# Four of the twelve output groups of the adaLN modulation computed on VectorE instead of TensorE

## The chip, the cores and the metric

One Trainium2 chip, one of its cores. The time is that of one execution on the device in microseconds (us), the median of the runs of a kernel. All data are float32, and the whole reference runs in one launch.

## The reference, cut to what matters

The program is a hybrid mixer block (gated linear attention, mLSTM, S5, SwiGLU) followed by two more layers (latent attention, LRU). The change touches the first step only: the modulation vector from the condition `c`, and beside it the first RMS norm.

```python
# c: (1, 1024), ada_w: (1024, 6144), ada_b: (6144,)
mod = silu(c) @ ada_w + ada_b            # six vectors of 1024: shift1, scale1, gate1, shift2, scale2, gate2
h = rms_norm(x, pre1_w) * (1 + scale1) + shift1       # x: (1024 tokens, 1024 features)
```

The product is a vector times a matrix of 25 MB. Only the first two of the six vectors (mod 0 to 15 below) are needed by the first norm; the others are used much later. Independent of both, keys and values of a memory of 256 tokens are computed from the input `mem_2`.

## The kernel before, in words

**Layout.** Features lie on the 128 partitions. `mod` is a tile of 128 x 48: column m holds outputs 128m to 128m+127. `ada_w` arrives in 48 slots of 512 KB. Slot n holds 256 rows of the matrix (k = 0, 1: two times 128 rows) for 512 columns; four slots make a group g = n // 4 of 512 outputs, which is four columns of `mod`. A ring `ada_w` holds eight slots.

**The product before.** DVE spreads silu(c) to `act0_wide` (L948), 128 equal columns for each block of 128 rows. TensorE multiplies (L932) each half slot by it, 128 x 128 stationary and 128 x 512 moving, and adds eight such products up in a PSUM bank (0 and 1 by turns). All 128 rows of the bank then hold the same 512 outputs. DVE multiplies them by the identity repeated four times (`pick`, L958) and sums along the free axis (L962) into four columns of `mod`. TensorE may enter the bank of group g only when the pick of group g - 2 is done. A float32 matmul stands in the trace as two MATMUL and two LDWEIGHTS rows, so that a slot is four rows of L932.

**What runs beside it.** `side_by_side` (L499) merges the programs of several parts into one instruction order for each engine: each `yield` names a due time, and instructions are issued in the order of due times; afterwards each engine follows that fixed order and waits on semaphores. S(n) = 8 + 1.9n is the due time of slot n and X(i) = S(2 + 5i) that of quarter i of x. The parts are these.

- `modulation()`: the above. SyncE issues the transfer of slot n when slot n - 8 has been used (`pe_done`).
- `first_slots()`: six slots of the ordinary weight ring `w`; ACT rounds four of them (L268), and GpSimd subtracts to get the rest (L277).
- `squares()`: four transfers of 1 MB of x (L1002), ACT squares (L1014), DVE adds up over the features (L1024), in two halves of 512 tokens.
- `statistic()` for each half: TensorE sums over the partitions with narrow products (L784: four products of 128 x 128 by 128 x 1), DVE and ACT make the root, and TensorE spreads it over a bank with two rows of L791.
- `normed()` for each half: DVE scales x (L1039), ACT adds the shift and rounds (L1051), DVE makes the rest (L1043), eight tiles each. It needs `fold`, which needs mod 0 to 15, groups 0 to 3.
- `memory_keys()`: when the last L1043 is done, since it lies over x, SyncE loads `mem` (L1073); ACT rounds (L1125), DVE makes the rest (L1151). TensorE's work on it (L285 with `mem_parts`) stands behind all 48 slots in TensorE's order.

The next stage begins when this block has ended on every engine.

**Lines that matter in the order of DVE.** Before the change, DVE's order from the pick of group 3 on is: that pick, mod and fold (L965, L953, L967), the last seven adds of L1024 among the sixteen pairs of L1039 and L1043, and a pick for each further group wherever its due time falls.

Of the kernel before, what the change touches and what calls it, by code (L numbers as in the profile page):

```python
# [24 lines left out]
ALU = mybir.AluOpType  # L25
AX = mybir.AxisListType

P = 128
# [3 lines left out]
HALF = 512  # L32
# [3 lines left out]
ADA_RING = 8  # L36
ADA_SLOTS = 48
# [94 lines left out]
def ordered(*programs):  # L132

    waiting = [[next(p, None), n, p] for n, p in enumerate(programs)]
    waiting = [w for w in waiting if w[0] is not None]
    while waiting:
        first = min(waiting, key=lambda w: w[:2])
        yield first[0]
        at = next(first[2], None)
        if at is None:  # L140
            waiting.remove(first)
        else:
            assert at >= first[0] - 1e-6, (at, first[0])
            first[0] = at
# [10 lines left out]
def build(nc, a):  # L155
    ctx = ExitStack()
    with ctx:
# [3 lines left out]
        def sb_in(scope, name, shape, dt=F32, high=False):  # L161

            names[name] = names.get(name, 0) + 1
            name = f"{name}_sb{names[name]}"
            size = -(-int(np.prod(shape[1:])) * 4 // 32) * 32
            edges = sorted(spans)
            holes = list(zip([SBUF_LO] + [e for _, e in edges], [b for b, _ in edges] + [SBUF_HI]))
            fits = [(lo, hi) for lo, hi in holes if hi - lo >= size]
            assert fits, (name, size, holes)
            at = (fits[-1][1] - size) // 32 * 32 if high else fits[0][0]  # L170
            span = (at, at + size)
            spans.append(span)
            scope.callback(spans.remove, span)
            return nc.alloc_sbuf_tensor_at(name, shape, dt, offset=at)
# [20 lines left out]
        def sem(name):  # L195
            return Count(ctx.enter_context(nc.semaphore(name)))
# [5 lines left out]
        def over(counts):  # L202

            for count, times in counts:
                spare.append(Count(count.sem, count.n + times))

        ps = ctx.enter_context(nc.psum_tensor("ps", [P, 8, HALF], F32))
# [7 lines left out]
        mod = sb("mod", [P, 48])  # L215
        fold = sb("fold", [P, 32])
        act0 = sb("act0", [P, 8])
# [9 lines left out]
        ident, ones = C("ident"), C("ones")  # L227
# [4 lines left out]
        pe_done = sem("pe_done")  # L232
        act_free = sem("act_free")
        dve_free = sem("dve_free")
        ada_full = [sem(f"ada_full{s}") for s in range(ADA_RING)]
# [658 lines left out]
        with ExitStack() as scope:  # L894
            ada_w = sb_in(scope, "ada_w", [P, ADA_RING, 2, HALF])
            pick = sb_in(scope, "ada_pick", [P, 4, P])
            act0_wide = sb_in(scope, "ada_silu", [P, DT, P])
# [4 lines left out]
            silu_s, wide_s, picked, fold_s = sem("ada_silu"), sem("ada_wide"), sem("ada_picked"), sem("ada_folded")  # L902
            x_s = [sem(f"x0_loaded{i}") for i in range(4)]
            sq_s, acc_s, scaled_s, hi_s, lo_s = (sem("norm1_squares"), sem("norm1_sums"), sem("norm1_scaled"),
                                                 sem("norm1_hi"), sem("norm1_lo"))
            base = pe_done.n

            S = lambda n: 8.0 + 1.9 * n
            X = lambda i: S(2 + 5 * i)

            def modulation():
                def on_sp(sp):
                    yield -10.0
                    sp.dma_start(vec[:], a["vec"]).then_inc(loaded.sem, 16)
                    sp.dma_start(cst[:], a["cst"]).then_inc(loaded.sem, 16)
                    for n in range(ADA_SLOTS):
                        yield S(n - ADA_RING) + 2.1
                        if n >= ADA_RING:
                            sp.wait_ge(pe_done.sem, base + n - ADA_RING + 1)
                        sp.dma_start(ada_w[:, n % ADA_RING].rearrange("p k m -> p (k m)"), a["ada"][n]  # L920
                                     ).then_inc(ada_full[n % ADA_RING].sem, 16)

                def on_pe(pe):
                    for n in range(ADA_SLOTS):
                        yield S(n)
                        if n == 0:
                            pe.wait_ge(wide_s.sem, 1)
                        if n % 4 == 0 and n >= 8:
                            pe.wait_ge(picked.sem, n // 4 - 1)
                        pe.wait_ge(ada_full[n % ADA_RING].sem, 16 * (n // ADA_RING + 1))  # L930
                        for k in range(2):
                            mm = nc.tensor.matmul(ps[:, n // 4 % 2], act0_wide[:, 2 * (n % 4) + k],  # L932
                                                  ada_w[:, n % ADA_RING, k], start=(n % 4 == 0 and k == 0),
                                                  stop=(n % 4 == 3 and k == 1))
                        mm.then_inc(pe_done.sem, 1)

                def on_act(act, link):
                    yield 0.0
                    act.wait_ge(loaded.sem, 32)
                    nc.scalar.activation(act0[:], V("c", 0, 8), ACT.Silu).then_inc(silu_s.sem, 1)  # L940
                    yield S(ADA_SLOTS)
                    act.wait_ge(pe_done.sem, base + ADA_SLOTS)
                    nc.scalar.activation(act0[:, 1:2], act0[:, 1:2], ACT.Copy).then_inc(act_free.sem, 8)

                def on_dve(dve, link):
                    yield 0.2
                    dve.wait_ge(silu_s.sem, 1)
                    nc.vector.tensor_copy(act0_wide[:], act0[:].unsqueeze(2).broadcast_to([P, DT, P])  # L948
                                          ).then_inc(wide_s.sem, 1)

                    def folded(weights):
                        for j, (w, m) in weights:
                            link(nc.vector.scalar_tensor_tensor(fold[:, 8 * j:8 * j + 8], mod[:, m:m + 8], 1.0, V(w, 0, 8),  # L953
                                                                ALU.add, ALU.mult))
                    for g in range(ADA_SLOTS // 4):
                        yield S(4 * g + 4) + 0.6
                        dve.wait_ge(pe_done.sem, base + 4 * g + 4)
                        nc.vector.tensor_tensor(pick[:], ps[:, g % 2].rearrange("p (j m) -> p j m", m=P),  # L958
                                                ident.unsqueeze(1).broadcast_to([P, 4, P]), ALU.mult
                                                ).then_inc(picked.sem, 1)  # L960
                        dve.wait_ge(picked.sem, g + 1)
                        link(nc.vector.tensor_reduce(mod[:, 4 * g:4 * g + 4], pick[:], AX.X, ALU.add))  # L962
                        if g == 3:

                            link(nc.vector.tensor_tensor(mod[:, 0:16], mod[:, 0:16], V("ada_b", 0, 16), ALU.add))  # L965
                            folded([(0, ("pre1_w", 8))])
                            nc.vector.tensor_copy(act0[:, 2:3], act0[:, 2:3]).then_inc(fold_s.sem, 1)  # L967
                    link(nc.vector.tensor_tensor(mod[:, 16:48], mod[:, 16:48], V("ada_b", 16, 32), ALU.add))
                    folded(enumerate([("post1_w", 16), ("pre2_w", 32), ("post2_w", 40)], 1))
                    nc.vector.memset(act0[:, 0:1], 0.0).then_inc(dve_free.sem, 8)  # L970
                return Part(on_sp, on_pe, on_act, on_dve)

            def first_slots():
                at = lambda n: S(8 + 4 * (n - RAW)) if n >= RAW else -1.0 + n
# [194 lines left out]
            for h in range(2):  # L1169
# [1 line left out]
                root = statistic(at, total[:, tokens(h)], [(acc_s.sem, 7 * h + 7)], (2 + h,), D, dg[:, h], st[:, h])  # L1171
                parts += [root, normed(h, max(at + 8.0, S(16) + 5.0), root.done, 2 + h)]
            side_by_side(modulation(), first_slots(), squares(), *parts)
            pe_done.n += ADA_SLOTS
            act_free.n += 8
            dve_free.n += 8
            loaded.n += 32
            stream["slot"] += 8
            kv_written.n += 64
            over([(mem_s, 16), (mem_hi, 8), (mem_lo, 8), (one_s, 2), (kv_t, 8), (slot_t, 0), (k_taken, 4), (v_taken, 4)])  # L1180
            over([(silu_s, 1), (wide_s, 1), (picked, ADA_SLOTS // 4), (fold_s, 1), (sq_s, 16), (acc_s, 14), (scaled_s, 16),
                  (hi_s, 16), (lo_s, 16), *((x, 16) for x in x_s)])
        x0_scope.close()
        kv_scope = ctx.enter_context(ExitStack())
# [1370 lines left out]
        with ExitStack() as scope:  # L2555
# [19 lines left out]
            def sums(dve, link):  # L2575
                for n, (m, hs) in enumerate(LATE_HALVES[1:], 1):
                    yield mixed.job_end[(m, hs)] + 0.8
                    cols = slice(hs[0] * HALF, (hs[-1] + 1) * HALF)
                    dve.wait_ge(*sq_s.at(n + 1))
                    if n > 1:  # L2580
                        dve.wait_ge(*acc_s.at(n - 1))
                    nc.vector.tensor_tensor(total[:, cols], total[:, cols], sq[:, n % 2, cols], ALU.add
                                            ).then_inc(acc_s.sem, 1)
# [1561 lines left out]
```

## Time and profile before

| | |
|---|---|
| median of three runs | 3388.56 us (3388.53 to 3395.3) |
| the profiled execution | 3396.56 us, of which the span from first to last instruction is 3394.4 us |
| granted TensorE clock, mean over the span | 0.940 |
| PE / DVE / ACT / POOL busy over the span | 91% / 39% / 29% / 24% |
| transfer of `ada_w` | 48 x 512 KB, median 6.6 us from issue to landing |

TensorE is busy nearly everywhere. The part of the program that is changed takes about the first 106 us of the span. PE, DVE, ACT, POOL and SP are TensorE, VectorE, ScalarE, GpSimd and SyncE; times in the rows are us from the span's start, mean durations of one instruction ns.

### The profile page before, as it was taken

The page shows a single profiled execution, that of the slowest core. Times are in us where ns is not written, and L with a number is a line of the kernel's source. Part 1 is how long each engine was busy: PE and PEld are TensorE (multiplying, and loading weights), DVE is VectorE, ACT ScalarE, POOL GpSimd, SP SyncE. Part 2 cuts the span into 40 slices and gives each one's busy share as a digit, 9 for nine tenths or more (in the row PEclk, how much of TensorE's full clock was granted, in tenths as well). Part 3 has the DMA queues.
Part 4 walks back from the last instruction along what each step waited for, and adds up shares of the span by engine and source line. Part 5 has one row for each costly group of instructions (what it writes and reads, how often), then busy time and mean ns, then how long its engine had stood idle before and what let it go on. Part 6 is the DMA issues. An engine that isn't in the chain of part 4 may idle for free. (4 is left out here: it accounts for less than half of the span.)

```text
span 3394.4 us, 33644 instructions
## 1 busy us (share of the span) xinstructions
PE 3078.6 (91%) x14024; PEld 2303.9 (68%) x14024; DVE 1318.3 (39%) x1342; ACT 975.2 (29%) x1262; POOL 813.6 (24%) x380
## 2 busy tenths in 40 slices
PE   8899999998989798899999999898699999888696
PEld 3677777876766476688888787675466666666455
DVE  5153111355325444300000345322556663538355
ACT  3132222212134123311111444232234331346212
POOL 1223112224232122322212345331112111133100
PEclk9899999999989898999999999998799999889898
DMA  9311111241132342111111233211100002120201
GB/s 350 135 50 63 50 50 62 106 167 69 62 131 90 110 171 67 53 43 49 44 49 46 78 130 106 96 62 71 62 13 20 13 19 75 50 81 29 86 13 50
DMA packets 76485, 261.01 MB, mean 77 GB/s; under 512 B 8048, under 2 KB 12384, under 8 KB 75328
## 3 DMA queue, kind: packets, MB, share of 16 engines
q1 hardware_dynamic: 76352, 259.13, 21.6%
q8 instruction: 97, 1.59, 0.2%
q14 instruction: 36, 0.29, 0.0%
HBM read 207.10 MB, written 51.99 MB: 76 GB/s over the span
## 5 line engine op out<-in xcount | busy, mean ns | idle before, releaser
L277 POOL TENSOR_TENSOR w_lo_sb<-raw_w_sb,w_hi_sb 128x1024 fp32r<-128x1024 f32 x231 | 577.8, 2502 | 2092.3 <-ACT w_hi_sb L268 2092.3
L268 ACT ACTIVATE w_hi_sb<-raw_w_sb 128x1024 fp32r<-128x1024 f32 x231 | 243.2, 1053 | 438.8 <-PE ps L285 405.8
L285 PE MATMUL ps<-merged_parts_hi_sb,w_hi_sb 128*128 128x512 f32 x832 | 333.1, 400 | 22.6 <-PEq L500 12.1
L285 PE MATMUL ps<-merged_parts_lo_sb,w_hi_sb 128*128 128x512 f32 x832 | 333.1, 400 | 0.0
L285 PE MATMUL ps<-h_hi_sb,w_hi_sb 128*128 128x512 f32 x720 | 294.7, 409 | 23.5 <-PEq L872 16.5
L285 PE MATMUL ps<-h_lo_sb,w_hi_sb 128*128 128x512 f32 x720 | 287.7, 400 | 0.0
L285 PE MATMUL ps<-merged_parts_hi_sb,w_lo_sb 128*128 128x512 f32 x832 | 274.7, 399 | 0.0
L285 PE MATMUL ps<-h_hi_sb,w_lo_sb 128*128 128x512 f32 x720 | 244.3, 399 | 0.0
L285 PE MATMUL ps<-z_lo,w_hi_sb 128*128 128x512 f32 x512 | 206.7, 404 | 0.0
L285 PEld LDWEIGHTS ps<-merged_parts_hi_sb,w_hi_sb 128*128 128x128 f32 x832 | 158.1, 190 | 68.9 <-issue 18.6
L2728 DVE TENSOR_TENSOR ffn_hidden_sb<-ffn_hidden_sb,ps 128x1024 f32 x20 | 24.4, 1221 | 431.4 <-PE ps L285 431.4
L285 PEld LDWEIGHTS ps<-merged_parts_lo_sb,w_hi_sb 128*128 128x128 f32 x832 | 158.2, 190 | 38.5 <-issue 0.5
L285 PEld LDWEIGHTS ps<-merged_parts_hi_sb,w_lo_sb 128*128 128x128 f32 x832 | 158.1, 190 | 37.5
L285 PE MATMUL ps<-z_hi,w_hi_sb 128*128 128x512 f32 x384 | 162.2, 423 | 19.8 <-POOL z_lo L3454 5.9
L285 PEld LDWEIGHTS ps<-h_hi_sb,w_hi_sb 128*128 128x128 f32 x720 | 137.3, 191 | 61.9 <-issue 27.3
L285 PEld LDWEIGHTS ps<-h_hi_sb,w_lo_sb 128*128 128x128 f32 x720 | 136.9, 190 | 33.7
L285 PEld LDWEIGHTS ps<-h_lo_sb,w_hi_sb 128*128 128x128 f32 x720 | 137.4, 191 | 31.8 <-issue 1.0
L285 PE MATMUL ps<-hid_hi_sb,w_hi_sb 128*128 128x512 f32 x352 | 141.0, 401 | 7.7 <-DVE hid_lo_sb L2823 7.7
L285 PE MATMUL ps<-hid_hi_sb,w_lo_sb 128*128 128x512 f32 x352 | 140.5, 399 | 0.0
L285 PE MATMUL ps<-hid_lo_sb,w_hi_sb 128*128 128x512 f32 x352 | 139.3, 396 | 0.0
L3174 PE MATMUL ps<-qh_sb,kh_sb 97*128 97x512 f32 (+3 forms) x288 | 125.3, 517 | 13.3 <-DMA qh_sb<-att_rows 10.7
L285 PE MATMUL ps<-z_hi,w_lo_sb 128*128 128x512 f32 x384 | 134.5, 404 | 0.0
(571 smaller groups left out, 5594.0 us busy)
## 6 DMA issues: line engine op xcount, KB each, us to landing
raw_w_sb<-in_w SPq DMA_DIRECT2D x231, 512.0 KB, 3.2
ada_w_sb<-in_ada SPq DMA_DIRECT2D x48, 512.0 KB, 6.6
inbox_sb<-gates_out SPq DMA_DIRECT2D x24, 512.0 KB, 3.9
gates_out<-outbox_sb SPq DMA_DIRECT2D x16, 512.0 KB, 2.6
inbox_sb<-sums_out SPq DMA_DIRECT2D x16, 512.0 KB, 4.7
spilled_sum<-x_sb SPq DMA_DIRECT2D x32, 256.0 KB, 2.0
x_sb<-spilled_sum SPq DMA_DIRECT2D x2, 4096.0 KB, 13.6
x_sb<-in_x SPq DMA_DIRECT2D x4, 1024.0 KB, 11.2
```

The source lines that it names most:

```text
L268: nc.scalar.activation(w_hi[:, n % RING].rearrange("p t m -> p (t m)"), raw_w[:, n % RAW], ACT.Copy).then_inc(w_rounded.sem, 1)
L277: nc.gpsimd.tensor_tensor(w_lo[:, n % RING].rearrange("p t m -> p (t m)"), raw_w[:, n % RAW], flat_hi, ALU.subtract).then_inc(w_split.sem, 1)
L285: mm = nc.tensor.matmul(o, wt, xs, start=start and part == 0 and xs is x_hi, stop=stop and part == 1)
L2728: return nc.vector.tensor_tensor(late[:, tile], late[:, tile], src, ALU.mult)
L3174: mm = nc.tensor.matmul(ps[:, 4 + n % 2, 0:hi - lo], k_of(u)[0:dq + 1, s * P:(s + 1) * P], q_of(u)[0:dq + 1, lo:hi], start=True, stop=not ...
```

## The change

Groups 2, 4, 6 and 8 (slots 8 to 11, 16 to 19, 24 to 27, 32 to 35) leave TensorE. For each of their slots DVE makes two instructions of 128 x 512: the weights times silu(c) as a scalar for each partition, added to a tile `scaled_w` (two buffers). The first of a group is a `tensor_scalar` without an addition, the other seven are `scalar_tensor_tensor`. DVE waits for its own result after each. When a group's eight products are added up, TensorE sums over the partitions with four narrow products by a column of ones into four columns of PSUM bank 5, and DVE copies these four columns to `mod`. SyncE waits for DVE (`dve_done`) where the slot that is replaced was DVE's.

The eight other groups stay as they were, with banks 0 and 1 by turns among themselves. The pick of group 3, 5, 7 and 9 has a due time not before that of the copy ahead of it.

```diff
+            on_vector = (2, 4, 6, 8)
+            by_pe = [n for n in range(ADA_SLOTS) if n // 4 not in on_vector]
+            by_dve = [n for n in range(ADA_SLOTS) if n // 4 in on_vector]
+            scaled_w = sb_in(scope, "ada_scaled", [P, 2, HALF])
@@ on_sp
-                        if n >= ADA_RING:
-                            sp.wait_ge(pe_done.sem, base + n - ADA_RING + 1)
+                        if n >= ADA_RING and n - ADA_RING in by_pe:
+                            sp.wait_ge(pe_done.sem, base + by_pe.index(n - ADA_RING) + 1)
+                        elif n >= ADA_RING:
+                            sp.wait_ge(dve_done.sem, by_dve.index(n - ADA_RING) + 1)
@@ on_pe
                         yield S(n)
+                        group = [g for g in range(ADA_SLOTS // 4) if g not in on_vector].index(n // 4) if n in by_pe else None
+                        if group is None:
+                            continue
...
+                def sums(pe):
+                    for j, g in enumerate(on_vector):
+                        yield S(4 * g + 4) + 7.0
+                        pe.wait_ge(dve_done.sem, 4 * j + 4)
+                        for m in range(4):
+                            mm = nc.tensor.matmul(ps[:, 5, 4 * j + m:4 * j + m + 1],
+                                                  scaled_w[:, j % 2, m * P:(m + 1) * P], ones[:, 0:1], start=True, stop=True)
+                        mm.then_inc(added_t.sem, 1)
@@ on_dve
+                    def products(j, g):
+                        for n in range(4 * g, 4 * g + 4):
+                            yield S(n) + 1.0
+                            dve.wait_ge(ada_full[n % ADA_RING].sem, 16 * (n // ADA_RING + 1))
+                            if n % 4 == 0 and j >= 2:
+                                dve.wait_ge(added_t.sem, j - 1)
+                            for k in range(2):
+                                c_k = act0[:, 2 * (n % 4) + k:2 * (n % 4) + k + 1]
+                                if n % 4 == 0 and k == 0:
+                                    ins = nc.vector.tensor_scalar(scaled_w[:, j % 2], ada_w[:, n % ADA_RING, k], c_k, None,
+                                                                  ALU.mult)
+                                else:
+                                    ins = nc.vector.scalar_tensor_tensor(scaled_w[:, j % 2], ada_w[:, n % ADA_RING, k], c_k,
+                                                                         scaled_w[:, j % 2], ALU.mult, ALU.add)
+                                if k == 0:
+                                    link(ins)
+                            ins.then_inc(dve_done.sem, 1)
+                            dve.wait_ge(dve_done.sem, by_dve.index(n) + 1)
...
+                        if g in on_vector:
+                            j = on_vector.index(g)
+                            yield from products(j, g)
+                            yield S(4 * g + 4) + 8.0
+                            dve.wait_ge(added_t.sem, j + 1)
+                            link(nc.vector.tensor_copy(mod[:, 4 * g:4 * g + 4], ps[:, 5, 4 * j:4 * j + 4]))
+                            continue
+                        group += 1
+                        yield max(S(4 * g + 4) + 0.6, S(4 * g) + 8.0 if g - 1 in on_vector else 0.0)
```

## Rows read from the trace of the kernel before

**Rows 1.** Timeline of PE: start, duration, line, operands, count, [idle before, releaser].
```profile
7.40 26.78 PE L932 MATMUL ps<-ada_w_sb,ada_silu_sb 128*128 128x512 f32 x56 [7.40 <-DMA ada_w_sb<-in_ada]
38.78 1.87 PE L784 MATMUL ps<-cst_sb,norm_total_sb 128*128 128x1 f32 x8 [4.60 <-DVE norm_total_sb L1024]
40.51 8.41 PE L932 MATMUL ps<-ada_w_sb,ada_silu_sb 128*128 128x512 f32 x12
...
63.12 1.05 PE L784 MATMUL ps<-cst_sb,norm_total_sb 128*128 128x1 f32 x8 [1.32 <-DVE norm_total_sb L1024]
64.03 5.40 PE L932 MATMUL ps<-ada_w_sb,ada_silu_sb 128*128 128x512 f32 x12
...
70.37 36.21 PE L932 MATMUL ps<-ada_w_sb,ada_silu_sb 128*128 128x512 f32 x84
106.02 0.68 PE L285 MATMUL ps<-mem_parts_hi_sb,w_hi_sb 128*128 128x256 f32 x1
```

**Rows 2.** Busy time by stretch: length, each engine (instructions), clock, DMA share, GB/s.
```profile
20.00:30.00 10.00, 10.00 (x25) 4.42 (x24) 3.36 (x5) 2.30 (x4) 0.00 (x0) 1.00 1.03 401
...
47.20:85.20 38.00, 36.68 (x92) 16.34 (x91) 34.02 (x55) 14.56 (x22) 0.94 (x1) 1.00 0.88 312
64.20:106.20 42.00, 42.00 (x99) 18.46 (x98) 30.65 (x52) 10.10 (x20) 0.00 (x0) 1.00 0.68 235
```

**Rows 3.** All transfers from 0 to 110 us.
```profile
DMA packets 10323, 34.35 MB, mean 312 GB/s; under 512 B 976, under 2 KB 1104, under 8 KB 10192
```

**Rows 4.** Timeline of DVE: columns as in rows 1.
```profile
17.05 0.69 DVE L958 TENSOR_TENSOR ada_pick_sb<-ps,cst_sb 128x512 f32<-128x512 f32 x1 [11.21 <-PE ps L932]
17.78 0.69 DVE L962 TENSOR_REDUCE mod_sb<-ada_pick_sb 128x4 f32<-128x512 f32 x1
...
32.66 2.28 DVE L1024 TENSOR_TENSOR norm_total_sb<-norm_total_sb,norm_sq_sb 128x512 f32<-128x512 f32 x3 [4.97 <-ACT norm_sq_sb L1014]
...
36.30 2.42 DVE L1024 TENSOR_TENSOR norm_total_sb<-norm_total_sb,norm_sq_sb 128x512 f32<-128x512 f32 x1
...
47.24 0.69 DVE L958 TENSOR_TENSOR ada_pick_sb<-ps,cst_sb 128x512 f32<-128x512 f32 x1 [5.22 <-PE ps L932]
...
83.11 2.07 DVE L1043 SCALAR_TENSOR_TENSOR h_lo_sb<-x_sb,mod_sb,h_hi_sb 128x512 fp32r<-128x512 f32 x3
```

**Rows 5.** Groups of DVE from 47.2 to 98.3 us: count, busy us, mean ns, idle before.
```profile
L1039 DVE SCALAR_TENSOR_TENSOR x_sb<-x_sb,fold_sb,ps 128x512 f32<-128x512 f32 x16 | 11.7, 743 | 0.1
L1043 DVE SCALAR_TENSOR_TENSOR h_lo_sb<-x_sb,mod_sb,h_hi_sb 128x512 fp32r<-128x512 f32 x16 | 11.7, 746 | 0.0
L958 DVE TENSOR_TENSOR ada_pick_sb<-ps,cst_sb 128x512 f32<-128x512 f32 x7 | 4.8, 689 | 9.6 <-PE ps L932 9.6
L1024 DVE TENSOR_TENSOR norm_total_sb<-norm_total_sb,norm_sq_sb 128x512 f32<-128x512 f32 x7 | 4.8, 687 | 0.3
```

**Rows 6.** Groups of DVE elsewhere: `tensor_scalar` and `scalar_tensor_tensor` over SBUF alone.
```profile
L1750 DVE TENSOR_SCALAR conv_box_sb<-ml_raw_sb,vec_sb 128x1024 f32<-128x1024 f32 x4 | 3.3, 813 | 19.8 <-ACT ml_raw_sb L1735 19.8
...
L2665 DVE SCALAR_TENSOR_TENSOR merged_parts_lo_sb<-half_scaled_sb,mod_sb,merged_parts_hi_sb 128x512 fp32r<-128x512 f32 x8 | 7.1, 886 | 0.0
```

**Rows 7.** Timeline of ACT: columns as in rows 1.
```profile
31.95 1.15 ACT L1014 ACTIVATE norm_sq_sb<-x_sb 128x512 f32<-128x512 f32 x2 [6.50 <-DMA x_sb<-in_x]
...
95.92 2.56 ACT L1125 ACTIVATE mem_parts_hi_sb<-mem_in 128x256 fp32r<-128x256 f32 x8 [11.96 <-DMA mem_in<-in_mem]
```

**Rows 8.** Timeline of POOL: columns as in rows 1.
```profile
35.84 2.34 POOL L277 TENSOR_TENSOR w_lo_sb<-raw_w_sb,w_hi_sb 128x1024 fp32r<-128x1024 f32 x1 [18.92 <-ACT w_hi_sb L268]
45.79 2.35 POOL L277 TENSOR_TENSOR w_lo_sb<-raw_w_sb,w_hi_sb 128x1024 fp32r<-128x1024 f32 x1 [7.61 <-ACT w_hi_sb L268]
```

**Rows 9.** The first L932 work of PE at the lower clock: columns as in rows 2.
```profile
36.50:46.50 10.00, 5.99 (x7) 0.50 1.03 403
```

**Rows 10.** Timeline of SP: issues, columns as in rows 1.
```profile
88.11 0.43 SPq L1073 DMA_DIRECT2D mem_in<-in_mem  x1
89.45 3.76 SPq L920 DMA_DIRECT2D ada_w_sb<-in_ada  x3
```

More of the change, by code:

```diff
@@ L908, in build @@
             S = lambda n: 8.0 + 1.9 * n
+            on_vector = (2, 4, 6, 8)
+            by_pe = [n for n in range(ADA_SLOTS) if n // 4 not in on_vector]
+            by_dve = [n for n in range(ADA_SLOTS) if n // 4 in on_vector]
+            scaled_w = sb_in(scope, "ada_scaled", [P, 2, HALF])
+            dve_done, added_t = sem("ada_dve"), sem("ada_added")
             X = lambda i: S(2 + 5 * i)
@@ L925, in on_pe @@
                         yield S(n)
+                        group = [g for g in range(ADA_SLOTS // 4) if g not in on_vector].index(n // 4) if n in by_pe else None
+                        if group is None:
+                            continue
                         if n == 0:
                             pe.wait_ge(wide_s.sem, 1)
-                        if n % 4 == 0 and n >= 8:
-                            pe.wait_ge(picked.sem, n // 4 - 1)
+                        if n % 4 == 0 and group >= 2:
+                            pe.wait_ge(picked.sem, group - 1)
                         pe.wait_ge(ada_full[n % ADA_RING].sem, 16 * (n // ADA_RING + 1))
                         for k in range(2):
-                            mm = nc.tensor.matmul(ps[:, n // 4 % 2], act0_wide[:, 2 * (n % 4) + k],
+                            mm = nc.tensor.matmul(ps[:, group % 2], act0_wide[:, 2 * (n % 4) + k],
                                                   ada_w[:, n % ADA_RING, k], start=(n % 4 == 0 and k == 0),
@@ L941, in on_act @@
                     yield S(ADA_SLOTS)
-                    act.wait_ge(pe_done.sem, base + ADA_SLOTS)
+                    act.wait_ge(pe_done.sem, base + len(by_pe))
                     nc.scalar.activation(act0[:, 1:2], act0[:, 1:2], ACT.Copy).then_inc(act_free.sem, 8)
@@ L954, in folded @@
                                                                 ALU.add, ALU.mult))
-                    for g in range(ADA_SLOTS // 4):
-                        yield S(4 * g + 4) + 0.6
-                        dve.wait_ge(pe_done.sem, base + 4 * g + 4)
-                        nc.vector.tensor_tensor(pick[:], ps[:, g % 2].rearrange("p (j m) -> p j m", m=P),
+                    def products(j, g):
[16 more added lines that the diff above has]
+                            dve.wait_ge(dve_done.sem, by_dve.index(n) + 1)
@@ new lines, in on_dve @@
+                    group = 0
+                    for g in range(ADA_SLOTS // 4):
+                        if g in on_vector:
[7 more added lines that the diff above has]
+                        yield max(S(4 * g + 4) + 0.6, S(4 * g) + 8.0 if g - 1 in on_vector else 0.0)
+                        dve.wait_ge(pe_done.sem, base + 4 * group)
+                        nc.vector.tensor_tensor(pick[:], ps[:, (group - 1) % 2].rearrange("p (j m) -> p j m", m=P),
@@ L959, in on_dve @@
                                                 ident.unsqueeze(1).broadcast_to([P, 4, P]), ALU.mult
                                                 ).then_inc(picked.sem, 1)
-                        dve.wait_ge(picked.sem, g + 1)
+                        dve.wait_ge(picked.sem, group)
                         link(nc.vector.tensor_reduce(mod[:, 4 * g:4 * g + 4], pick[:], AX.X, ALU.add))
@@ L970, in on_dve @@
                     nc.vector.memset(act0[:, 0:1], 0.0).then_inc(dve_free.sem, 8)
-                return Part(on_sp, on_pe, on_act, on_dve)
+                return Part(on_sp, lambda pe: ordered(on_pe(pe), sums(pe)), on_act, on_dve)
             def first_slots():
@@ L1173, in build @@
             side_by_side(modulation(), first_slots(), squares(), *parts)
-            pe_done.n += ADA_SLOTS
+            pe_done.n += len(by_pe)
             act_free.n += 8
@@ L1180, in build @@
             over([(mem_s, 16), (mem_hi, 8), (mem_lo, 8), (one_s, 2), (kv_t, 8), (slot_t, 0), (k_taken, 4), (v_taken, 4)])
-            over([(silu_s, 1), (wide_s, 1), (picked, ADA_SLOTS // 4), (fold_s, 1), (sq_s, 16), (acc_s, 14), (scaled_s, 16),
+            over([(silu_s, 1), (wide_s, 1), (picked, ADA_SLOTS // 4 - len(on_vector)), (fold_s, 1), (dve_done, len(by_dve)),
+                  (added_t, len(on_vector)), (sq_s, 16), (acc_s, 14), (scaled_s, 16),
                   (hi_s, 16), (lo_s, 16), *((x, 16) for x in x_s)])
```

## The prediction, made before the changed kernel was run

> **What bounds the kernel now.** I read the timeline of PE first, from the start to the first product of the memory's keys. That product, L285 on `mem_parts`, stands behind all 48 slots in PE's order and starts at 106.02 us [rows 1]; everything later hangs on it. Its other inputs are long there: ACT rounds `mem` from 95.92 [rows 7]. So the whole change is worth what it does to that 106.0. From 70.37 on PE runs 84 rows of L932 without a gap, 21 slots in 36.2 us: 1.72 us a slot [rows 1]. Between 64.2 and 106.2 PE is busy all the time while DVE is busy 30.65 of 42 us and the transfers use 235 GB/s [rows 2]. There PE is the bound. Earlier it isn't alone: PE waits 4.60 us for the sum of squares and then works at the lower clock, 1.2 of 2.4 GHz, granted 0.50 [rows 1, 9]; the transfers run at some 400 GB/s [rows 2]; and from 47.2 to 85.2 us DVE is busy 34.0 of 38 us [rows 2]. That last row is the one that decides here.
>
> **PE: what goes and comes.** Sixteen slots at 1.72 us leave: 27.5 us. Four batches of four narrow products come. The trace has the same batch as L784: 0.91 us from its start to the next row at the higher clock (63.12 to 64.03), 1.73 at the lower (38.78 to 40.51) [rows 1]. I take 0.9 to 1.8 each, 4 to 7 in all. If PE were the only bound, the keys would start 20 to 23 us earlier, between 83 and 86.
>
> **Transfers.** They put a floor under that. 34.35 MB pass up to 110 us [rows 3]; at 401 GB/s [rows 2] that is 86 us, and with some 3 us before the first and the last slot's 1.7 on PE nothing could start before about 90. The most that can be won is therefore 16 us, unless DVE is in the way.
>
> **DVE: the cost of the products.** One `scalar_tensor_tensor` of 128 x 512 takes 0.745 us (L1043, also two tiles of SBUF) [rows 5]. Here each waits for its own result; such a pair in the trace, L958 and L962, starts 0.73 apart for 0.69 each [rows 4], so I add 0.04: 0.785. The `tensor_scalar` takes 0.81 at 1024 columns [rows 6], so between 0.41 and 0.81 here; I take 0.49 with its wait, near the half. A group costs 0.5 + 7 x 0.785 = 6.0 us and a copy of 0.2 (estimate from the small operations around 0.2), and saves a pick and a reduce, 1.45. Four groups: +24.8 - 5.8 = +19 us on DVE. For the range: at 0.886 each, as L2665 [rows 6], a group is 7.0; at the fast price of `tensor_scalar` for all eight it would be 3.6.
>
> **The walk up to DVE's bottleneck.** PE ends slot 7 near 23.8 (6 slots before 34.18, the end of the first row [rows 1]) and must wait for slot 12, whose transfer ends only near 28, since it is some three transfers of 1.3 us ahead of the quarter of x that lands at 31.95 [rows 7]. So PE pauses for 4 us, does 12 and 13, and waits again for the sum of squares. On DVE slots 8 to 10 fall into the idle 4.97 us before 32.66 [rows 4] and cost nothing. Slot 11 lies among the four adds that follow: 32.66 + 4 x 0.73 + 1.57 = 37.1. That is earlier than before, where the last add took 2.42 us beside a POOL subtraction [rows 4, 8]. The narrow batch, slots 14 and 15 at the lower clock for most of it (3.4 us each against 1.7) and the sum of group 2 end near 45.5. DVE copies group 2 and picks group 3 from 45.6, where before it picked at 47.24 [rows 4].
>
> From there on DVE's order up to the last product of slot 35 holds: a copy, pick, reduce and three small operations of mod and fold 2.15; three groups of products 18.0; seven adds at 0.73, 5.1; sixteen L1039 and fifteen L1043 at 0.66 from start to start (83.11 to 85.18 are three [rows 4]), 20.5; two copies 0.4; two picks with reduce 2.9; the root and the diagonal of the second half 1.1. The sum is 50.15. The only gap I find is 1.1 us in front of the copy of group 4: the second half's narrow batch waits for DVE's last add and the sum of group 4 behind it, at the lower clock. 45.6 + 50.15 + 1.1 = 96.9. In the same order before, the last L1043 ended at 85.2 [rows 4].
>
> **What that does to PE.** The due times put the sum of group 8, S(36) + 7 = 83.4, ahead of slot 40 (84.0). So PE, which is through with slot 39 near 93, stands still until DVE has finished slot 35 at 96.9. Then come the sum, 0.9, and slots 40 to 47, 13.7: the keys start at 111.5 at the full clock. Behind the 4.60 us of waiting in the trace PE had the lower clock until 46.5 [rows 1, 9], which cost it some 3.9 us of work. Here the wait is about 4 us; I take a part of that loss, 2.5 us, and get 114.0. Against 106.0 that is +8.0.
>
> The Trainium skill (TensorE: Matmul & The Clock Gate, What's actually happening) says the throttled state is the default and that activity releases it; the trace's 0.50 behind the wait of 4.60 us agrees. By it alone every one of the new waits of PE costs twice: the time and the clock after it.
>
> **What is hidden.** SyncE now waits for DVE before slots 16 to 19 and so on. These issues come 3 us later than before, but the queue is full up to about 36 us, and later rings are refilled before PE asks, since PE's own slots are free early. What stands behind such a wait in SyncE's order is the load of `mem`: it waits for the last L1043 anyway, goes out near 98 where it was issued at 88.11 [rows 10], and lands near 105, as it took 7.8 us [rows 7, 10]. ACT's and DVE's parts of it follow within 3 us, before 114. If PE had not been held up, this would be the next bound, at about 106: the first of these parts gates the keys. GpSimd's two subtractions near 36 and 46 [rows 8] fall beside waiting DVE in my walk.
>
> On that last point the Trainium skill (SBUF — State Buffer, SBUF: two separate sides) has a rule that speaks against the change: a DVE operation with two inputs in SBUF and a GpSimd operation that reads SBUF exclude each other for the whole instruction. The last add beside L277, 2.42 us against 0.69, agrees. The seven products of a group have such inputs, the matmuls they replace did not.
>
> The shift of the keys is carried to the end: what follows, down to the next stage, is released by PE's products themselves. The profiled execution of 3396.56 us, a span of 3394.4 and 2.2 around it, would become 3404.6. It stands 8.0 above the median of the runs, so the difference is put on the median: 3388.56 + 8.0 = 3396.6 us. A measurement of this kernel tells about 0.2% from nothing, 6.8 us.
>
> **The rivals.**
> A. *As above, DVE's order is the bound.* 3396.6, own range 3393.5 to 3400. For it: DVE's 34 of 38 us [rows 2] before 19 us are added.
> B. *The same, but PE keeps its clock.* Slots 14 and 15 run 3 us earlier, nothing is lost after slot 35: keys at 109.4, 3392. Against it: the waits in PE's order are as long as the one that cost the clock before.
> C. *Faster: DVE's gaps swallow the products and PE's 27 us are won.* It needs keys before 99.2 to be seen. Between 64.2 and 106.2 DVE has 11.4 us idle [rows 2], but most of it lies behind the norm. Even at 3.6 us a group the walk of DVE's order ends 7.2 us earlier, 89.7, and the keys start at 104.3 to 106.5, no change. Only if products cost next to nothing, under some 0.2 each, do they start near 97 to 101, PE's own work with its early waits: 3380 to 3384. It decides by the duration of one product.
> D. *Heavier: the products run long.* At 0.93 each, start to start, from 0.886 [rows 6] or because GpSimd's subtractions are caught (2.4 us each by the long add, twice), the 24 instructions in the bottleneck add 3.5 to 5 us, and PE's second wait and the clock after it lengthen: keys at 118 to 119, 3401.
> E. *Not what it says:* the planner's order lets PE pass, for instance because due times tie otherwise than I read; 3388, no change.
>
> **Chances.** A 0.52, B 0.16, C 0.08 (half of it seen as faster), D 0.18, E 0.06. Slower than 3395.3: most of A (0.43), D and 0.01 of the rest, 0.62. Faster than 3381.8: 0.04. No difference: 0.34. The range from B's lower part to beyond D, 3389 to 3403, leaves out C, part of E and the far end of D.
>
> **What would show it.** After: a row of PE waiting near 93 to 97 for DVE's `ada_scaled`, the first L285 at 112 to 116; DVE without gaps from 46 to 97; products 0.745 each; PE's clock at 0.50 near 98 to 102. Idle DVE between 50 and 90, or a start of L285 before 107, would make the prediction wrong; so would a wait of the keys for `mem`.

## The result, and the profile after

The first five runs of the changed kernel had a median of 3408.0 us (3406.3 to 3413.3) against 3393.3 of five of the kernel before: ratio 1.0044, interval 1.0027 to 1.0060. The kernel was run twice more in the study (ratios 1.0029, 1.0012 to 1.0045, and 1.0035, 1.0020 to 1.0050). All 29 runs have a mean of 3404.2 (standard error 1.0), all 139 of the kernel before 3392.2 (0.5). The change costs 11.9 us, +- 2.3 (95%). The forecast was +8.0 on 3388.56, which is 3396.6, with a range of 3389 to 3403: slower, as forecast, and by more. The profiled execution took 3408.01, its span is 3406.2.

The timeline of PE in the changed kernel, with the columns of [rows 1], which it answers:

```profile
7.52 15.50 PE L943 MATMUL ps<-ada_w_sb,ada_silu_sb 128*128 128x512 f32 x32 [7.52 <-DMA ada_w_sb<-in_ada]
28.16 5.12 PE L943 MATMUL ps<-ada_w_sb,ada_silu_sb 128*128 128x512 f32 x8 [5.14 <-DMA ada_w_sb<-in_ada]
37.27 1.32 PE L784 MATMUL ps<-cst_sb,norm_total_sb 128*128 128x1 f32 x8 [4.00 <-DVE norm_total_sb L1073]
...
64.89 1.87 PE L784 MATMUL ps<-cst_sb,norm_total_sb 128*128 128x1 f32 x8 [11.42 <-DVE norm_total_sb L1073]
66.62 1.84 PE L954 MATMUL ps<-cst_sb,ada_scaled_sb 128*128 128x1 f32 x8
73.74 2.08 PE L791 MATMUL ps<-norm_diag_sb,cst_sb 128*128 128x512 f32 x2 [5.27 <-DVE norm_diag_sb L795]
...
97.24 1.86 PE L954 MATMUL ps<-cst_sb,ada_scaled_sb 128*128 128x1 f32 x8 [5.22 <-DVE ada_scaled_sb L988]
98.97 15.86 PE L943 MATMUL ps<-ada_w_sb,ada_silu_sb 128*128 128x512 f32 x32
114.26 0.68 PE L285 MATMUL ps<-mem_parts_hi_sb,w_hi_sb 128*128 128x256 f32 x1
```

The keys start at 114.26, 8.2 us later than at 106.02 [rows 1]. PE has three new long gaps: it waits 11.42 us for the second half's sum of squares (1.32 before), 5.27 for the diagonal, and 5.22 in front of the sum of group 8, released by DVE's last product.

Busy time by stretch in the changed kernel (columns of [rows 2]):

```profile
44.30:97.20 52.90, 29.96 (x77) 14.82 (x76) 50.33 (x77) 16.16 (x26) 2.35 (x1) 0.79 0.70 258
58.40:78.90 20.50, 8.73 (x22) 5.68 (x23) 19.06 (x32) 6.96 (x12) 0.00 (x0) 0.50 0.56 209
95.90:102.80 6.90, 5.56 (x13) 3.49 (x14) 5.74 (x8) 0.00 (x0) 0.00 (x0) 0.51 0.84 308
```

DVE (third pair) is busy 50.3 of the 52.9 us between the copy of group 2 and the last product; PE 30.0. PE's granted clock is 0.50 and 0.51 in the second and third of these stretches, which take in the late part of a long wait and what follows it. The groups of DVE from 44.3 to 98 us, columns of [rows 5]:

```profile
L988 DVE SCALAR_TENSOR_TENSOR ada_scaled_sb<-ada_w_sb,act_sb,ada_scaled_sb 128x512 f32<-128x512 f32 x21 | 15.8, 750 | 0.5
L1014 DVE TENSOR_TENSOR mod_sb<-mod_sb,vec_sb 128x16 f32<-128x16 f32 x1 | 2.2, 2244 | 0.0
L985 DVE TENSOR_SCALAR ada_scaled_sb<-ada_w_sb,act_sb 128x512 f32<-128x512 f32 x3 | 1.4, 483 | 0.1
```

A product takes 0.750 us (0.745 was taken), the first of a group 0.483. The add of 16 columns (L1014) took 2.24 us where it took 0.175 in the kernel before. It ended 0.03 us behind a subtraction of GpSimd that had begun before it. In the second trace of the changed kernel (e4 below) the add began later and took 0.58 us, and again ended 0.03 us behind GpSimd. First the rows of the changed kernel, then those of e4:

```profile
44.37 0.16 DVE L1002 COPY mod_sb<-ps 128x4 f32<-128x4 f32 x1 [4.16 <-PE ps L954]
46.02 2.24 DVE L1014 TENSOR_TENSOR mod_sb<-mod_sb,vec_sb 128x16 f32<-128x16 f32 x1
45.88 2.35 POOL L277 TENSOR_TENSOR w_lo_sb<-raw_w_sb,w_hi_sb 128x1024 fp32r<-128x1024 f32 x1 [6.22 <-ACT w_hi_sb L268]
```
```profile
47.18 0.58 DVE L1014 TENSOR_TENSOR mod_sb<-mod_sb,vec_sb 128x16 f32<-128x16 f32 x1
45.37 2.36 POOL L277 TENSOR_TENSOR w_lo_sb<-raw_w_sb,w_hi_sb 128x1024 fp32r<-128x1024 f32 x1 [6.23 <-ACT w_hi_sb L268]
```

So the time at which DVE could go on to `fold` was set there by GpSimd's subtraction and not by the copy of group 2.

After the keys two smaller losses come. The key and value work up to GpSimd's twelfth subtraction takes 29.2 us from the keys' start (28.5 before): +0.7. Then PE starts the next stage, 9.0 us later than before, and stays at the lower clock for 5.8 us against 3.0. The first row is of the changed kernel, the second of the kernel before:

```profile
154.89:160.70 5.81, 5.81 (x14) 4.61 (x15) 0.00 (x0) 0.00 (x0) 0.00 (x0) 0.50 0.28 95
```
```profile
145.89:148.90 3.01, 3.01 (x7) 2.43 (x8) 0.00 (x0) 0.00 (x0) 0.00 (x0) 0.50 0.56 182
```

GpSimd's twentieth subtraction L277 is a mark that both kernels pass, here first in the changed kernel, then before:

```profile
274.24 3.15 POOL L277 TENSOR_TENSOR w_lo_sb<-raw_w_sb,w_hi_sb 128x1024 fp32r<-128x1024 f32 x1 [3.58 <-ACT w_hi_sb L268]
```
```profile
262.37 3.14 POOL L277 TENSOR_TENSOR w_lo_sb<-raw_w_sb,w_hi_sb 128x1024 fp32r<-128x1024 f32 x1 [3.58 <-ACT w_hi_sb L268]
```

That is 119.35 us behind the restart (PE's first product of the next stage) against 116.48, 2.9 more. 8.2 + 0.7 + 2.9 = 11.8 for this pair of traces. That it comes so near the 11.9 of the runs is partly luck: from that mark to the end the traces of the changed kernel alone differ by up to 8 us, and the runs of the kernel before lie between 3378.6 and 3404.9.

### The profile page after: what moved, and what is told of

The parts are those of the page before. It is cut to its first block and busy times, and to the rows that moved or that the text cites. A ratio compares the mean times of both kernels' runs of the same rounds, so it can differ in the third digit from the quotient of the medians.

```text
span 3406.2 us, 33618 instructions
## 1 busy us (share of the span) xinstructions
PE 3061.3 (90%) x13992; PEld 2299.1 (67%) x13992; DVE 1334.7 (39%) x1370; ACT 975.3 (29%) x1262; POOL 814.1 (24%) x380
## 5 line engine op out<-in xcount | busy, mean ns | idle before, releaser
L277 POOL TENSOR_TENSOR w_lo_sb<-raw_w_sb,w_hi_sb 128x1024 fp32r<-128x1024 f32 x231 | 578.7, 2506 | 2098.8 <-ACT w_hi_sb L268 2098.8
```

Of the source, the lines that this page charges most:

```text
L277: nc.gpsimd.tensor_tensor(w_lo[:, n % RING].rearrange("p t m -> p (t m)"), raw_w[:, n % RAW], flat_hi, ALU.subtract).then_inc(w_split.sem, 1)
```

## The experiments

Each had 12 timed runs beside 29 to 35 of the kernel before. "Mean" below is the difference of the means, with the standard error of the experiment's own mean.

Times in the rows count from the start of each trace, and the traces don't start alike: PE's first product stands at 7.40 in the kernel before, at 7.52 in the changed one, and between 6.5 and 8.1 in the others. Keys are therefore compared from that first product. So counted they start at 98.6 in the kernel before and at 106.7, 106.7, 106.9 and 106.5 in the four traces with the changed kernel's stage (e4, e10 and e11 below are the others). Differences under 1 us mean nothing here: up to the second half's narrow batch, traces of kernels that are the same to that point differ by that much.

**e1_short_products.** DVE's products over 64 of 512 columns. This leaves out seven eighths of four groups' products.

```diff
-ins = nc.vector.tensor_scalar(scaled_w[:, j % 2], ada_w[:, n % ADA_RING, k], c_k, None, ALU.mult)
+ins = nc.vector.tensor_scalar(scaled_w[:, j % 2, 0:64], ada_w[:, n % ADA_RING, k, 0:64], c_k, None, ALU.mult)
...  # the same for scalar_tensor_tensor; the sum's stationary operand is `ones`, four products as before
```

> Leaves out seven eighths of DVE's products: each of the 32 works on 64 of 512 columns (the four columns of mod of each such group come out wrong), all waits, transfers and the order of every engine stay, and the four narrow products of a sum stay four. Theory (DVE's order is the bound of the stage): a product then costs about 0.2 us instead of 0.785, the chain from the copy of group 2 to the last product of slot 35 shrinks from 51 us to about 37, the wait of PE in front of the sum of group 8 vanishes, and the keys start at 100 to 104 instead of 114.3; total against the kernel before between -6 and 0 us (ratio 0.998 to 1.000). Rival (PE's added waits come from the order and the narrow products, whatever a DVE product costs): keys stay within 3 us of 114.3, ratio 1.003 to 1.005.

Ratio 0.9987 (0.9973 to 1.0002), mean -1.7 +- 1.5. The timeline of PE:

```profile
61.96 1.87 PE L784 MATMUL ps<-cst_sb,norm_total_sb 128*128 128x1 f32 x8 [7.91 <-DVE norm_total_sb L1073]
88.86 1.05 PE L954 MATMUL ps<-ada_scaled_sb,cst_sb 128*128 128x1 f32 x8 [0.56 <-DVE ada_scaled_sb L988]
100.32 5.42 PE L943 MATMUL ps<-ada_w_sb,ada_silu_sb 128*128 128x512 f32 x12 [1.34 <-DMA ada_w_sb<-in_ada]
105.17 0.68 PE L285 MATMUL ps<-mem_parts_hi_sb,w_hi_sb 128*128 128x256 f32 x1
```

The wait for the last product is 0.56 instead of 5.22. Counted from the first product the keys start at 97.1, which is 9.6 us earlier than in the changed kernel, and the whole cost is gone: DVE's time makes it. But 105.2 is later than the 100 to 104 expected. A short product takes 0.283 us, not 0.2, PE still waits 7.91 us for the second half's squares, and behind the vanished wait stands the next bound, a transfer (1.34). Of the 27.5 us that PE was relieved of, no more than some 1.5 are won.

**e2_late_sum.** The sum of group 8 behind slot 47.

```diff
-yield S(4 * g + 4) + 7.0
+yield S(4 * g + 4) + 7.0 if g < 8 else S(ADA_SLOTS) - 0.5     # sum into bank 2, copy behind the pick of group 10
```

> The sum of group 8 moved behind slot 47 in PE's order (into bank 2), its copy behind the pick of group 10; nothing left out. Theory (the wait in front of slot 40 is a wait of order: PE stands behind DVE's last product although slots 40 to 42 have landed or soon land): PE goes on with slots 40 to 42 at once and waits at slot 43, whose transfer starts only when slot 35 has been used (97.3) and lands near 101; keys at 109 to 112, total 2 to 5 us below the changed kernel (ratio to the kernel before about 1.003). Rival (the ring, not the order, holds PE): slot 43 is as late as the sum was, keys at 113 to 115, no difference from the changed kernel (1.004).

Keys at 111.44, which is 104.9 from the first product and 1.8 us earlier than in the changed kernel. At least 2.3 had been expected, and the rival had up to 1.3: it lies between them. PE runs slots 40 to 44 one by one, 40 to 43 behind a transfer each (the rows of 41 to 43 are shown) and 44 behind a pick of DVE:

```profile
94.29 1.98 PE L943 MATMUL ps<-ada_w_sb,ada_silu_sb 128*128 128x512 f32 x4 [0.82 <-DMA ada_w_sb<-in_ada]
97.17 1.98 PE L943 MATMUL ps<-ada_w_sb,ada_silu_sb 128*128 128x512 f32 x4 [0.90 <-DMA ada_w_sb<-in_ada]
99.85 1.98 PE L943 MATMUL ps<-ada_w_sb,ada_silu_sb 128*128 128x512 f32 x4 [0.69 <-DMA ada_w_sb<-in_ada]
111.44 0.37 PE L285 MATMUL ps<-mem_parts_hi_sb,w_hi_sb 128*128 128x256 f32 x1
```

So 1.8 us of the 8.2 are order. The rest I put down to DVE's time reaching PE over the ring, since these slots' transfers had to wait for slots that DVE uses; no run tests this by itself. In the runs the gain can't be seen: ratio 1.0029 (1.0017 to 1.0041), mean +12.2 +- 0.9.

**e3_warm_waits.** Extra products on PE in its two long waits.

```diff
+if g in (4, 8):
+    yield X(3) + 11.9 if g == 4 else S(4 * g + 4) + 6.9
+    for _ in range(11 if g == 4 else 5):
+        nc.tensor.matmul(ps[:, 7], act0_wide[:, 0], act0_wide[:, 0:4].rearrange("p a m -> p (a m)"), start=True, stop=True)
```

> The changed kernel with 11 extra products on PE in front of the second half's narrow batch and 5 in front of the sum of group 8 (0.86 us each at the full clock, into bank 7, used by nobody there): they fill PE's two long waits of 11.4 and 5.2 us. Theory (the lower clock behind the waits costs 3 to 4 us of the 8.2): granted clock 1.00 at 65 and at 98 to 103, copy of group 4 about 1 us earlier, keys at 110 to 112, 2.5 to 4 us below the changed kernel. Rival (DVE alone sets it, the clock costs nothing on the path): keys within 1 us of 114.3.

```profile
64.94 1.03 PE L959 MATMUL ps<-cst_sb,ada_scaled_sb 128*128 128x1 f32 x8
95.34 1.05 PE L959 MATMUL ps<-cst_sb,ada_scaled_sb 128*128 128x1 f32 x8 [0.43 <-DVE ada_scaled_sb L993]
96.25 13.98 PE L943 MATMUL ps<-ada_w_sb,ada_silu_sb 128*128 128x512 f32 x32
109.67 0.68 PE L285 MATMUL ps<-mem_parts_hi_sb,w_hi_sb 128*128 128x256 f32 x1
```

Sums at 1.03 instead of 1.84, the last eight slots in 13.98 instead of 15.86 us. The keys at 109.67 are 103.1 from the first product, 3.7 us earlier than in the changed kernel, as expected (2.5 to 4). Ratio 1.0013 (0.9997 to 1.0029), mean +5.6 +- 1.6. Of the 8.2 us, 3.7 are the lower clock that the waits bring, some 4.5 DVE's order itself. The granted clock behind the restart of the next stage was low for 3.6 us here, and the mark lay 116.7 behind it.

**d10_delay.** The kernel before with ten extra products between slot 47 and the keys, the same call as in e3.

> The kernel before with ten extra products on PE (512 columns, bank 7, 0.86 us each: 8.6 us) between slot 47 and the first product of the keys: a pure shift of all that follows, about the size of the one the change makes (8.2 us). Theory (a shift is carried to the end one for one): +8.6 us, ratio 1.0020 to 1.0031. Rival (the shift changes where PE's waits and the clock's changes meet, and the rest adds some 3.5 us as in the changed kernel's trace): +11 to +13 us, ratio 1.0033 to 1.0040.

Keys at 114.64; ratio 1.0024 (1.0009 to 1.0038), mean +9.0 +- 1.3 for the 8.6 us of products. A shift alone is carried about one for one, as the theory had it; its restart kept the lower clock 4.0 us, and the twentieth subtraction lay 115.7 behind it.

**e4_after_again and e10_after_third.** The changed kernel, unaltered.

> The changed kernel itself again, unaltered, with more runs beside the kernel before. Its stage costs 8.2 us in the trace, its first five runs gave a ratio of 1.0044 (14.9 us). Theory (a shift is carried one for one, as the delayed kernel before showed with +8.5 for 8.6; the rest was the scatter of few runs): ratio 1.0018 to 1.0032. Rival (the change costs some 6 us more further on): ratio 1.0038 to 1.0048 again.

> The changed kernel unaltered beside them. Theory (8.2 us at the keys, carried one for one): ratio 1.0018 to 1.0032, and with the seventeen runs so far a mean of about 1.003. Rival (a further cost of some 6 us): 1.0038 or more again.

Ratios 1.0029 and 1.0035, means +10.3 +- 1.7 and +11.6 +- 1.4. The first is in the theory's range, the second between the two. All 29 runs together cost 11.9 us, 3.7 more than the shift of 8.2 and outside the interval of +- 2.3. Without the first five runs, which had raised the question, and against the kernel before as run beside them, the excess is 2.8 +- 2.6 (95%): most likely real, and not 6 us. Keys at 113.6 and 114.4; lower clock behind the restart 5.6 and 5.7 us; the mark at 119.2 and 119.3.

**e5_group2_only, e6_group4_only, e7_group11_only.** One group on DVE, at three places of its order.

```diff
-on_vector = (2, 4, 6, 8)
+on_vector = (2,)    # e5;  (4,) in e6;  (11,) in e7, sum in bank 3
+act.wait_ge(dve_done.sem, len(by_dve))    # before ACT's last operation on act0
```

> Only group 2 on DVE. Theory (what counts is where in DVE's order the products fall): they fall into DVE's idle time between 27.7 and 33 us and cost nothing; PE's saved 6.9 us fall in front of its wait for the sum of squares and win nothing: keys at 105 to 107.5 (before 106.0), ratio 0.9993 to 1.0006. Rival (each group moved costs a quarter of the total): +2 us.

> Only group 4 on DVE, in the stretch from 47 to 58 us where DVE is busiest. Theory: the 6 us of products less 1.45 delay the sum of squares of the second half and everything behind it on DVE; PE waits for that sum in front of its narrow batch some 5 to 7 us instead of 1.3, gives back its 6.9 us and loses clock behind the wait: keys at 107.5 to 112, ratio 1.0005 to 1.0018. Rival (each group a quarter): the same +2 us as with group 2.

> Only the last group, 11, on DVE (its sum goes to bank 3, behind the first products of the keys in PE's order; the last wait of ACT is for DVE's products too). DVE is idle more than half of the time from 86 to 106 us and PE is busy throughout. Theory: PE loses four slots, 6.9 us, nothing waits for DVE: keys at 99 to 101, ratio 0.9975 to 0.9985, below both kernels. Rival (each group moved costs 2 us): ratio 1.0006. Third: the transfers or mem hold the keys, at 102 to 105, ratio 0.9990 to 0.9998.

The first product of the keys, in e5, e6 and e7:

```profile
105.81 0.68 PE L285 MATMUL ps<-mem_parts_hi_sb,w_hi_sb 128*128 128x256 f32 x1
```
```profile
111.39 0.68 PE L285 MATMUL ps<-mem_parts_hi_sb,w_hi_sb 128*128 128x256 f32 x1
```
```profile
98.69 0.68 PE L285 MATMUL ps<-mem_parts_hi_sb,w_hi_sb 128*128 128x256 f32 x1
```

Counted from the first product the keys are at 98.6, 104.9 and 91.3, against 98.6 before. The same work moved costs 0, +6.3 or -7.3 us there, by its place in DVE's order. In e6 PE waits 10.60 us for the second half's squares. The runs: e5 1.0007 (0.9991 to 1.0022), mean +2.6 +- 1.5, no clear difference; e6 1.0032 (1.0014 to 1.0049), mean +10.3 +- 2.1, more than the +1.7 to 6 us expected; e7 1.0006 (0.9991 to 1.0022), mean +2.2 +- 1.9, so the gain at the keys did not arrive. Group 4 alone costs 6.3 of the 8.2 us at the keys and nearly what all four cost in the runs: products in front of the second half's sum of squares, for which PE waits, do most of the harm. ACT shows why e7 gained nothing:

```profile
106.86 0.20 ACT L965 ACTIVATE act_sb<-act_sb 128x1 f32<-128x1 f32 x1 [8.70 <-DVE ada_scaled_sb L989]
```

This small operation now waits for DVE's last product, and the rounding of the next weights stands behind it.

**e8_group11_free_act, e9_group11_again.** That operation moved 26 us down in ACT's order.

> As the kernel with only group 11 on DVE, with ACT's last small operation of the modulation (which waits for DVE's last product) moved behind ACT's work on the keys. In the run before, the keys started at 98.7 instead of 106.0 but ACT stood at that wait until 106.9 and GpSimd's first subtraction behind it was only 2.5 us earlier than in the kernel before. Theory: with the wait out of the way the 7.3 us reach that subtraction (6.5 to 7.5 us earlier, near 104) and the end: ratio 0.9974 to 0.9986, 5 to 9 us below the kernel before. Rival (the rest of the block, the ring's transfers or the copy of the values, takes the gain back): under 3 us earlier at GpSimd's fourth subtraction, ratio 0.9992 to 1.0005.

> The same kernel once more in the same call, for a narrower interval (one median of twelve runs scatters by some 3 us here): as the run beside it, the two medians within 4 us.

Ratios 0.9993 (0.9981 to 1.0005) and 0.9998 (0.9986 to 1.0010), means -0.4 both: the rival's range. Counted from the first product, GpSimd's fifth subtraction was 7.9 us earlier than in the kernel before, as the theory had it, but the twelfth only 3.0 (1.6 in e9). The wait had moved on, to PE, which stands at the sum for DVE's last product, at the lower clock behind it:

```profile
109.52 1.87 PE L954 MATMUL ps<-cst_sb,ada_scaled_sb 128*128 128x1 f32 x8 [2.99 <-DVE ada_scaled_sb L989]
```

**e11_after_warm_end, e12_before_warm_end.** 18 extra products behind the last product of the values, in both kernels.

```diff
+yield kv_at + 8 * step + 3.0
+for _ in range(18):
+    nc.tensor.matmul(ps[:, 0], act0_wide[:, 0], act0_wide[:, 0:4].rearrange("p a m -> p (a m)"), start=True, stop=True)
```

> The changed kernel with 18 extra products on PE (512 columns, bank 0) behind the last product of the values, where PE waits some 17 us for the block's end. In three traces of the changed kernel PE starts the next stage at the lower clock and keeps it 5.6 to 5.9 us, in the kernel before 3.1; GpSimd's twentieth subtraction then lies 119.3 against 116.5 us behind that start. Theory (that clock is 2.8 of the changed kernel's 12 us): full clock at the start of the next stage, the subtraction 113 to 115 us behind it, mean time 3 to 6 us below the changed kernel's 3404.2, ratio to the kernel before 1.0015 to 1.0026. Rival (the loss lies elsewhere): the subtraction at 118 or more, ratio 1.003 to 1.0038.

> The same 18 products in the kernel before. Theory: full clock at the start of the next stage, the twentieth subtraction 113 to 115 us behind it instead of 116.5; ratio 0.9988 to 0.9998 (1.5 to 3 us less). Rival: no effect, or products that hold up the block's end: ratio 1.000 or more.

```profile
153.78:157.00 3.22, 3.22 (x14) 2.63 (x15) 0.00 (x0) 0.00 (x0) 0.00 (x0) 1.00 0.54 170
```

The clock is 1.00 at the restart (row of e11), and the mark lies 113.95 and 113.96 us behind it, as the theory had it: 5.4 us less than in the changed kernel, 2.5 less than in the one before. Ratios 1.0013 (0.9999 to 1.0026) and 0.9988 (0.9976 to 0.9999); means -6.2 against the changed kernel's 3404.2 and -4.4 +- 0.9. With both restarts at the full clock the kernels are 9.9 us apart (standard error 1.9), near the 8.2 between the restarts of these two traces. What the lower clock behind a restart costs up to the mark is shown by the traces, 2.5 us in the one and 5.4 in the other. That it cost the changed kernel more over all its runs is not: the two effects in the means differ by 1.8 with a standard error of 2.2.

**e13_group11_late_sum, e14_group11_warm_end.** Only group 11 on DVE, ACT's operation moved as in e8, sum and copy 20 us later in their orders; then with the 18 products as well.

```diff
-yield S(4 * g + 4) + 7.0
+yield S(4 * g + 4) + 27.0
```

> Only group 11 on DVE, its sum and copy moved behind the work on the keys on PE and DVE (in the run before PE waited 3.0 us in front of that sum, and 8.6 us won at GpSimd's fifth subtraction were 3.6 by the eighth). Theory (nothing on PE waits for DVE any more): keys at 97 to 100, the twelfth subtraction 28.5 to 29.5 us behind them, 6 to 8 us earlier than in the kernel before, ratio 0.9974 to 0.9986. Rival (the ring's transfers take it back): under 4 us at the twelfth subtraction, 0.9988 to 1.0.

> The same with the 18 products at the block's end: both gains add, ratio 0.9965 to 0.9982; rival: only one of them shows, 0.9982 to 0.9992.

Keys at 98.40 and the twelfth subtraction 29.1 us behind: PE waits for DVE nowhere on the way. e13: 0.9988 (0.9975 to 1.0002), mean -5.3 +- 1.4; the theory's times in the trace were met, its ratio (up to 0.9986) just missed. Its restart had the lower clock for 6.1 us. e14: 0.9982 (0.9969 to 0.9996), mean -6.6 +- 1.3, median 3386.6: some 0.2% faster than the kernel before. If the gains of e13 and e12 added, it would be -9.7; the difference is within the errors.

## Why the prediction was right in its mechanism and short in its size

- *Bound and order.* Right. DVE has hardly a gap from the copy of group 2 to the last product of slot 35, and e1, e5 and e6 show that its time there decides. The end of slot 35, 97.2 for a forecast 96.9, is nearer than the working deserves. DVE restarted at 44.37 and not at 45.6, since slots 14 and 15 took 4.9 us instead of up to 3.4 each. From there to the end of slot 35 it needed 52.8 us and not 50.15 + 1.1. The add of 16 columns behind GpSimd's subtraction brought 2.1 us that the walk had left out, since it put both subtractions beside a waiting DVE; the rest was 0.5 shorter. The two errors cancel because GpSimd's subtraction, and not the restart, set when DVE went on: in e4 DVE restarted at 45.53, the add took 0.58 us, and slot 35 was done, counted from the first product, within 0.1 us of the same time.
- *Price of a product.* Right: 0.750 us for 0.745. The gap in front of the copy of group 4 was 0.95 (1.1).
- *PE behind slot 35.* Sum, eight slots and 2.5 us of clock gave 114.0; 114.26 was measured. PE was through with slot 39 at 92.0 (93) and waited 5.2 us (4). The clock's share in the whole stage is 3.7 us by e3: the first wait of 11 us counts too, since the sums and the spread behind it are on DVE's path.
- *The step that failed:* "The shift of the keys is carried to the end: what follows ... is released by PE's products themselves", and with it the sum +8.0. It is 8.2 at the keys and 11.9 at the end. 0.7 to 1.0 goes to the key and value work (29.2 to 29.5 us in the four traces of the changed kernel's stage, 28.3 to 28.6 in the kernel before, e12 and d10); why, no run shows. 2.9 goes, in the traces, to the restart of PE behind 17 us of waiting, at the lower clock for 5.6 to 5.9 us in all three traces of the changed kernel instead of 3.0. d10's trace shows that a delay by itself need not bring it. Whether the change brings it is open, and the other traces speak against a simple link. e5, with its keys where they were before, had 5.3 us and its mark 119.1 behind the restart; e13, with its keys 7 us earlier, had 6.1 and 119.4. e1, e2, e3 and e6, with products on DVE too, had 3.6 to 4.8 us and 115.8 to 116.7. And e2, with 4.2 us and 115.9, still cost 12.2 us in its runs. So the 8.2 at the keys has a shown cause, and of the 3.7 behind them the runs leave the larger part open.
- *The base.* The +8.0 was put on a median of three runs, 3388.56. 139 runs have a median of 3392.6. That is 4 of the 8 us between the forecast of 3396.6 and the pooled 3404.5, and no matter of the change. The first five runs of the changed kernel, 3408.0, lay 3.5 above the pooled median in addition.
- *Rival D* (3401, products longer) came near in time and wrongly in cause. The products were not longer. Of its other cause, GpSimd's subtractions, one did hold DVE up, by 2.1 us. *C* asked for products under 0.2 us; they took 0.750. e1 bears out the forecast's step below it: at 0.283 us a product the keys come at 105.2, where 104.3 to 106.5 had been said for 3.6 us a group.

## What to carry to other kernels

Work moved from a full engine to one that is 39% busy is not free: read the busy share of the stretch and, in the receiving engine's fixed order, what stands behind the place where it is put. The same work, one group of twelve, cost -7, 0 or +6 us at the keys by its place. An engine relieved and then made to wait pays twice, for the wait and for the clock behind it (3.7 of 8.2 us here). Two traces are compared from a common event and not from their starts, which here differ by up to 1.5 us. And where runs scatter by 26 us, three of them are no base for a forecast of 8.

## What was not expected of the hardware

Eighteen idle products in a wait of 17 us at the end of a stage, the clock then being 1.00 instead of 0.50 at the restart, took 4.4 us (ratio 0.9988, 0.9976 to 0.9999) off the kernel before, without any of its own work touched. A `tensor_tensor` of only 16 columns beside GpSimd's subtraction took 2.24 us instead of 0.175, nearly as long as one of 512 columns (2.42 [rows 4]). It took 1.49, 0.58 and 0.55 where it began later in the subtraction (e1, e4, e3) and ended 0.03 us behind it each time: what it pays is the rest of GpSimd's operation, not a price of its own size.
